# Hybrid attention and expert layer on one core: weights split earlier, squares moved a stage ahead, expert rows loaded ahead, h turned first

## The chip, the cores and the metric

The kernel runs on one core of one Trainium2 chip. The time is the device time of one execution in microseconds; the figure quoted is the median of the runs. One further execution was recorded by the hardware profiler, and every row below is from it.

## What is computed

One layer over 512 tokens of width 1024, in float32: a token mixer with two head groups and one output projection, then a retrieval of single-neuron experts. Cut to what matters here:

```python
h = rms(x) * (1 + scale1) + shift1
proj = h @ w_in
sb_out  = head_rms(stick_breaking_attention(...), 8 heads) * g_sb
gla_out = head_rms(gla_chunked(...), 4 heads) * g_gla * silu(g_r)     # gated linear attention
mixed = concatenate([sb_out, gla_out]) @ w_out
x = x + gate1 * mixed
h2 = rms(x) * (1 + scale2) + shift2
q = h2 @ w_peer_q                        # 8 heads x (128 + 128)
s1, s2 = q1 . keys_a, q2 . keys_b        # 128 keys each; top 16 of each, then top 16 of the pairs
act = gelu(h2 . expert_u[idx]);  y = sum(gates * act * expert_v[idx])
x = x + gate2 * y;  out = rms(x) * g_final
```

128 tokens get their experts by gathered rows; for the other 384 all 16384 expert rows are multiplied (128 blocks of 128 rows), and the picked ones are weighted.

## The kernel before

All data lie transposed in SBUF: 128 partitions of channels by 512 tokens, eight channel blocks (KD = 8, TB = 4 of them from each head group). Matrix products are made in three passes on a split of each float32 operand: hi is the value rounded to the matmul type fp32r, lo the remainder, and the passes are hi*hi, hi*lo, lo*hi. Every split costs a copy on ScalarE (hi) and a subtraction on VectorE or GpSimd (lo).

Every engine has its own queue, written out by hand in program order; engines meet by semaphores. The front of the kernel is a chain of blocks (`nc.Block()`), and all engines meet at the end of each. Around the change they are:

- stick-breaking attention (to 273 us), whose SyncE queue loads all of w_out (L623).
- `gated_linear` (273.7 to 295): TensorE sums squares of the attention output (`head_sums`, L817) for its norm, makes chunk scores (L827), state updates (L847) and outputs (L858, L864). ScalarE makes four squares, four logarithms (L774) and four exponentials (L777) for the norm; a third head sum has to wait for the first logarithm, as there are two banks. VectorE masks scores (L789), keeps the state, and at the end copies the four gated outputs from PSUM to catT (L809). GpSimd makes the mask.
- `mixer_back` (295 to 373): norm of the gated outputs (ScalarE squares L920, TensorE sums L975, ScalarE Ln and Exp L926, L928, VectorE L1020 and the gate L1022), then hi and lo of the concatenation (L923, L930, L934; `cat_low`, L1012), then the output projection: eight tiles n of eight blocks k of three matmuls (L986 to L988), tiles 0 and 1 interleaved by halves (`spans`). Its weights are split tile by tile into a ring of three buffers, hi by ScalarE (`w_high`, L917), lo by GpSimd (L966). VectorE adds each tile to x (L1029), ScalarE squares it (L943), VectorE adds the squares up (L1035, L1038). At the end the sum over channels (L994, L996), Ln and Exp (L948, L950), then for each k: VectorE scales (L1044), ScalarE makes h_hi (L955) and a full copy (L958), VectorE h_lo (L1048). TensorE then makes the first head's two query halves (L1002 to L1004), for which GpSimd splits the weights (L969) behind ScalarE's hi (L946, L951). These weights are loaded into the spent front of catT when cat_lo is done (L907).
- `retrieval` (373 on), within one block with everything that follows: SyncE loads keys, the first two expert blocks, the next query weights, more expert blocks (a ring of four, `UpProducts.load`, L1078). TensorE makes the key scores (L1297), turns the first 128 tokens of h (L1305, L1306), and then walks through 128 expert blocks (`product`, 24 matmuls each, L1103 to L1105), with the next head's query product (`query_of`, L1285) and scores between them. An expert block's hi is ScalarE's (L1086), its lo VectorE's (L1093, before VectorE's top-16 turn for blocks 0 and 1, within the turns for the others). GpSimd splits the next query weights (L1271) when the scores of the head before are copied (L1339), and then gathers expert rows for the indices that the turn has found (L1162).

The projections' buffer t16 has 16 slots of 512 columns. Slots 0 to 11 (queries and keys of both head groups) are spent when the gated stage's operands are made; slots 12 to 15 hold the gate, read at L1022.

## Time and profile before

| | us |
|---|---|
| median of three runs | 1639.35 |
| range of the runs | 1638.86 to 1641.07 |
| the profiled execution | 1643.19 |
| its span in the trace | 1641.5 |

| engine | busy us | share of the span |
|---|---|---|
| TensorE matmul (PE) | 1563.1 | 95% |
| TensorE weight load (PEld) | 1376.5 | 84% |
| VectorE (DVE) | 1290.5 | 79% |
| ScalarE (ACT) | 713.9 | 43% |
| GpSimd (POOL) | 392.6 | 24% |

How to read it: rows of a timeline give the start, the duration, the engine, the line of the kernel, the operation with out<-in, shape and count, and in brackets how long the engine had been idle and who ended that.
### The profile page before, as it was taken

How to read it: one execution, taken by the hardware profiler on the slowest of the kernel's cores; microseconds unless marked ns; L12 is line 12 of the kernel's file. 1: busy time of each engine (PE TensorE's matmuls, PEld its weight loads, DVE VectorE, ACT ScalarE, POOL GpSimd, SP SyncE). 2: the span in 40 equal slices, each digit the busy share in tenths (PEclk: the TensorE clock that was granted, in tenths of full speed). 3: DMA queues.
4: the chain of work that ended last, by engine and by line, in shares of the span. 5: the costliest groups of instructions: out<-in, count | busy, mean ns of one | idle time of the engine just before them, and what ended most of it. 6: DMA issues, size and time to landing. Idle time of an engine off the chain costs nothing.

```text
span 1641.5 us, 23626 instructions
## 1 busy us (share of the span) xinstructions
PE 1563.1 (95%) x8161; PEld 1376.5 (84%) x8161; DVE 1290.5 (79%) x2612; ACT 713.9 (43%) x1124; POOL 392.6 (24%) x328
## 2 busy tenths in 40 slices
PE   5899988889999999999999999999999999999996
PEld 3687656668899999999999999998888888888885
DVE  6665375546598999999999999747888888888888
ACT  4222384443343434334477677634333333333333
POOL 0000000321432333233222222102333333333330
PEclk8899988999999999999999999999999999999998
DMA  8573300005768887888889899879999999999992
GB/s 318 210 276 146 116 14 0 27 0 198 273 206 270 284 278 241 286 256 279 288 268 319 317 325 318 320 254 335 343 350 358 352 356 356 354 351 356 350 358 94
DMA packets 176963, 426.83 MB, mean 260 GB/s; under 512 B 15168, under 2 KB 99280, under 8 KB 172112
## 3 DMA queue, kind: packets, MB, share of 16 engines
q1 hardware_dynamic: 139984, 291.14, 50.7%
q0 software_dynamic: 36864, 134.23, 23.7%
q8 instruction: 63, 1.03, 0.2%
q14 instruction: 52, 0.43, 0.1%
HBM read 372.88 MB, written 52.43 MB: 259 GB/s over the span
## 4 chain that ended last, share of the span: by engine, by line
PE 72%; DVE 1%; issue 0%; ACT 0%; DVEq 0%; ACTq 0%
PE ps_y L1886 10%; PE ps_y L1888 10%; PE ps_y L1890 10%; PE ps_u L1103 10%; PE ps_u L1105 10%; PE ps_u L1104 10%; PE ps_g L1598 5%; PE ps_q L1285 1%; PE ps_q L1287 1%; PE ps_q L1286 1%; PE ps_s L1297 1%; DVE y_scaled L1861 0%; DVE row L1868 0%; PE ps_u L1910 0%; DVE y_row L1182 0%
## 5 line engine op out<-in xcount | busy, mean ns | idle before, releaser
L1103 PE MATMUL ps_u<-h_hi,u_hi 128*128 128x384 f32 x1024 | 348.8, 341 | 1.7 <-DVE u_lo L1093 1.7
L1105 PE MATMUL ps_u<-h_hi,u_lo 128*128 128x384 f32 x1024 | 345.0, 337 | 0.0
L1104 PE MATMUL ps_u<-h_lo,u_hi 128*128 128x384 f32 x1024 | 344.8, 337 | 0.0
L1765 ACT CAST v_hi<-v_raw 128x1024 fp32r<-128x1024 f32 x128 | 134.7, 1052 | 327.4 <-issue 327.4
L1162 POOL DMA_INDIRECT row<-in_v,row_index x128 | 176.8, 1381 | 401.5 <-DVE y_row L1182 308.0
L1162 POOL DMA_INDIRECT row<-in_u_rows,row_index x128 | 151.0, 1180 | 448.3 <-DVE row_dots L1169 377.6
L1822 DVE TENSOR_TENSOR v_lo<-v_raw,v_hi 128x1024 fp32r<-128x1024 f32 x128 | 160.6, 1255 | 103.2 <-ACT v_hi L1765 103.2
L1886 PE MATMUL ps_y<-v_hi,w_hi 128*128 128x512 f32 x768 | 237.3, 390 | 0.0
L1888 PE MATMUL ps_y<-v_lo,w_hi 128*128 128x512 f32 x768 | 236.6, 389 | 0.0
L1890 PE MATMUL ps_y<-v_hi,w_lo 128*128 128x512 f32 x768 | 236.5, 389 | 0.0
L1093 DVE TENSOR_TENSOR u_lo<-u_raw,u_hi 128x1024 fp32r<-128x1024 f32 x128 | 167.0, 1311 | 78.1 <-ACT u_hi L1086 78.0
L1103 PEld LDWEIGHTS ps_u<-h_hi,u_hi 128*128 128x128 f32 x1024 | 193.3, 189 | 2.4 <-DVE u_lo L1093 1.8
L1104 PEld LDWEIGHTS ps_u<-h_lo,u_hi 128*128 128x128 f32 x1024 | 193.1, 189 | 0.6
L1105 PEld LDWEIGHTS ps_u<-h_hi,u_lo 128*128 128x128 f32 x1024 | 193.0, 188 | 0.0
L1890 PEld LDWEIGHTS ps_y<-v_hi,w_lo 128*128 128x128 f32 x768 | 144.1, 188 | 30.1
L1888 PEld LDWEIGHTS ps_y<-v_lo,w_hi 128*128 128x128 f32 x768 | 144.1, 188 | 30.1
L1886 PEld LDWEIGHTS ps_y<-v_hi,w_hi 128*128 128x128 f32 x768 | 143.4, 188 | 29.2
L1113 ACT ACTIVATE u_act<-ps_u 128x384 f32<-128x384 f32 x128 | 62.8, 490 | 232.4 <-PE ps_u L1105 221.9
L1182 DVE SCALAR_TENSOR_TENSOR y_row<-row,row_weights,y_row 128x1024 f32<-128x1024 f32 x126 | 160.6, 1276 | 0.0
L1169 DVE CUSTOM_DVE_ANT_0 row<-row,h_row 128x1024 f32<-128x1024 f32 x128 | 155.3, 1217 | 1.8 <-DMA row<-in_u_rows,row_index 1.8
L1086 ACT CAST u_hi<-u_raw 128x1024 fp32r<-128x1024 f32 x128 | 134.1, 1048 | 3.2 <-DMA u_raw<-in_u 3.2
L1598 PE MATMUL ps_g<-hot_i,hot_j 128*128 128x128 f32 x768 | 91.9, 275 | 0.0
(284 smaller groups left out, 2325.9 us busy)
## 6 DMA issues: line engine op xcount, KB each, us to landing
u_raw<-in_u SPq DMA_DIRECT2D x128, 512.0 KB
v_raw<-in_v SPq DMA_DIRECT2D x128, 512.0 KB
w_ada<-in_w_ada SPq DMA_DIRECT2D x24, 1024.0 KB, 6.4
activations<-u_act SPq DMA_DIRECT2D x128, 192.0 KB
gate_tiles<-g_tile SPq DMA_DIRECT2D x12, 2048.0 KB
gates<-gate_tiles SPq DMA_DIRECT2D x32, 768.0 KB
act<-activations SPq DMA_DIRECT2D x128, 192.0 KB
w_proj<-in_w_proj SPq DMA_DIRECT2D x16, 512.0 KB, 3.9
```

Of the source, the lines that this page charges most:

```text
L1093: dve.tensor_tensor(self.lo[n][:], self.raw[n][:], self.hi[n][:].bitcast(F32), ALU.subtract).then_inc(self.lo_done, 1)
L1103: pe.matmul(out, self.hi[n][:, k], hi, start=(k == 0), stop=False)
L1104: pe.matmul(out, self.hi[n][:, k], lo, start=False, stop=False)
L1105: last = pe.matmul(out, self.lo[n][:, k], hi, start=False, stop=(k == KD - 1))
L1162: pool.indirect_dma_start(out=self.row[n][:], out_offset=None, in_=self.table[q // PICKS], in_offset=bass.IndirectOffsetOnAxis(ap=self.ind ...
L1169: dve.tensor_tensor_reduce(self.row[n][:], self.row[n][:], h_row[:], 1.0, 0.0, ALU.mult, ALU.add, self.dots[:, q:q + 1])\
L1182: dve.scalar_tensor_tensor(y, self.row[n][:], col, y, ALU.mult, ALU.add).then_inc(self.row_used, 1)
L1598: last = pe.matmul(ps_g[m][:, o], hot_j[x % HB][:, slot], hot_i[x % HB][:, slot], start=True, stop=True)
L1822: dve.tensor_tensor(v_lo[i % VS][:], v_raw[i % VS][:], v_hi[i % VS][:].bitcast(F32), ALU.subtract).then_inc(vlo, 1)
L1886: pe.matmul(out, hi, v_hi[i % VS][:, c], start=first, stop=False)
L1888: pe.matmul(out, hi, v_lo[i % VS][:, c], start=False, stop=False)
L1890: last = pe.matmul(out, lo, v_hi[i % VS][:, c], start=False, stop=end)
```

## The change

- **Two weight tiles split ahead.** Eight buffers of one weight tile each (`keep["split"]`) are laid over t16. In `gated_linear`, ScalarE copies the hi of out-projection tiles 0 and 1 between its squares and its logarithms, GpSimd subtracts their lo. `mixer_back` uses these four buffers as its ring, which has two places now instead of three; tile n's hi waits for product n - 2.
- **Squares a stage earlier.** ScalarE squares the gated outputs from PSUM at the end of `gated_linear`, two before and two after VectorE's copies of the same banks, and VectorE copies heads 2 and 3 first.
- **First query weights.** Their hi and lo go into buffers 4 to 7. ScalarE's copies stand in tiles 2 and 3 of the projection, and the lo is VectorE's now, not GpSimd's.
- **Order of the query product.** Per k the two hi*hi and lo*hi pairs wait for h_hi alone; the pair with h_lo follows.
- **cat_low(2, 4)** comes behind the first gated channel on VectorE.
- **Expert blocks 0 to 3** are loaded in `mixer_back`, behind the query weights in SyncE's queue; in `retrieval` the next query weights directly follow the keys.
- **h turned first**, before the first scores; ScalarE makes the hi of expert blocks 0 and 1 before it copies the scores.

```diff
         ps_o = [pb(f"ps_gla_o{h}", [P, T]) for h in range(GLA_HEADS)]
-        zeros = sem("gla_block_zeros")
+        w_hi, w_lo = keep["split"][0:2], keep["split"][2:4]
+        zeros, whi, squared, o_kept = sem("gla_block_zeros"), sem("w_out_first_hi"), sem("gla_o_squared"), sem("gla_o_kept")
...
             pool.memset(causal[0:C, C:P], 0.0).then_inc(zeros, 1)
+            for n in range(2):
+                pool.wait_ge(whi, n + 1)
+                pool.tensor_tensor(w_lo[n][:], keep["w_out"][:, n], w_hi[n][:].bitcast(F32), ALU.subtract)
...
                 act.activation(sq[:, c], catT[:, c], ACT.Square).then_inc(sq_done, 1)
+            act.wait_ge(keep["w_out_in"], 16)
+            for n in range(2):
+                act.copy(w_hi[n][:], keep["w_out"][:, n]).then_inc(whi, 1)
...
                 act.activation(rstd[:, c], rstd[:, c], ACT.Exp, scale=-0.5).then_inc(rstd_done, 1)
+            for p in range(GLA_PAIRS):
+                if p == 0:
+                    act.wait_ge(o_done, 2)
+                else:
+                    act.wait_ge(o_kept, 2)
+                for h in (2 * p, 2 * p + 1):
+                    act.activation(v8[:, 0, h], ps_o[h][:], ACT.Square).then_inc(squared, 1)
...
                     dve.scalar_tensor_tensor(catT[:, n], catT[:, n], keep["gains"][:, n:n + 1], rstd[:, n], ALU.mult, ALU.mult)
-            for h in range(GLA_HEADS):
-                dve.wait_ge(o_done, h // 2 * 2 + 2)
-                dve.tensor_copy(catT[:, TB + h], ps_o[h][:])
+            for p in reversed(range(GLA_PAIRS)):
+                if p == 0:
+                    dve.wait_ge(squared, 2)
+                else:
+                    dve.wait_ge(o_done, GLA_HEADS)
+                for h in (2 * p, 2 * p + 1):
+                    dve.tensor_copy(catT[:, TB + h], ps_o[h][:]).then_inc(o_kept, 1)
...
-def mixer_back(nc, io, keep, t16, v8, gx, catT, query):
+def mixer_back(nc, io, keep, t16, v8, gx, catT, query, up):
...
         h_hi, h_lo = keep["h_hi"], keep["h_lo"]
-        WS = 3
+        WS = 2
...
         cat_hi, cat_lo = sb("cat_hi", [P, KD, T], F32R), sb("cat_lo", [P, KD, T], F32R)
-        w_hi = [sb(f"w_out_hi{n}", [P, KD, P], F32R) for n in range(WS)]
-        w_lo = [sb(f"w_out_lo{n}", [P, KD, P], F32R) for n in range(WS)]
+        w_hi, w_lo = keep["split"][0:2], keep["split"][2:4]
...
         halves = lambda tile: [tile[:, 2 * s:2 * s + 2].rearrange("p a (b c) -> p (a b) c", c=P) for s in range(2)]
-        wq, wq_hi, wq_lo = halves(catT), halves(cat_hi), halves(cat_lo)
+        wq = halves(catT)
+        wq_hi, wq_lo = [keep["split"][n] for n in (4, 6)], [keep["split"][n] for n in (5, 7)]
...
         ps_x = pb("ps_sum_2", [P, T])
-        sq_done, sum_done, ln_done, rstd_done = sem("hsq"), sem("hsum"), sem("hln"), sem("hrstd")
+        sum_done, ln_done, rstd_done = sem("hsum"), sem("hln"), sem("hrstd")
...
                 sp.dma_start(wq[s], io["w_q"][s]).then_inc(wq_in, 16)
+            for b in range(up.RING):
+                up.load(sp, b)
...
             def w_high(n):
-                if n == 0:
-                    act.wait_ge(keep["w_out_in"], 16)
-                if n >= WS:
-                    act.wait_ge(mix_done, n - WS + 1)
-                    act.wait_ge(wlo, n - WS + 1)
+                act.wait_ge(mix_done, n - WS + 1)
...
-            for c in range(NG):
-                act.activation(sq[:, c], catT[:, TB + c], ACT.Square).then_inc(sq_done, 1)
-                if c == 1:
-                    w_high(0)
-                    act.copy(cat_hi[:, 0:2], catT[:, 0:2]).then_inc(chi, 2)
+            act.copy(cat_hi[:, 0:2], catT[:, 0:2]).then_inc(chi, 2)
...
                     act.copy(cat_hi[:, 2:4], catT[:, 2:4]).then_inc(chi, 2)
-                    w_high(1)
...
             for n in range(KD):
-                if n + 2 < KD:
-                    w_high(n + 2)
+                if n + WS < KD:
+                    w_high(n + WS)
...
                 act.activation(sq[:, n % 2], xT[:, n], ACT.Square).then_inc(sq2_done, 1)
-            act.wait_ge(wq_in, 32)
-            act.wait_ge(mix_done, KD)
-            act.copy(wq_hi[0], wq[0]).then_inc(query["hi"], 1)
+                if 2 <= n < 4:
+                    act.wait_ge(wq_in, 32)
+                    act.copy(wq_hi[n - 2][:], wq[n - 2]).then_inc(query["hi"], 1)
...
             act.activation(rstd[:, 0], rstd[:, 0], ACT.Exp, scale=-0.5).then_inc(rstd2_done, 1)
-            act.copy(wq_hi[1], wq[1]).then_inc(query["hi"], 1)
...
         def _(pool):
-            for n in range(KD):
-                pool.wait_ge(whi, n + 1)
-                if n >= WS:
-                    pool.wait_ge(mix_done, n - WS + 1)
+            for n in range(WS, KD):
+                pool.wait_ge(whi, n - WS + 1)
+                pool.wait_ge(mix_done, n - WS + 1)
                 pool.tensor_tensor(w_lo[n % WS][:], keep["w_out"][:, n], w_hi[n % WS][:].bitcast(F32), ALU.subtract).then_inc(wlo, 1)
-            for s in range(2):
-                pool.wait_ge(query["hi"], s + 1)
-                pool.tensor_tensor(wq_lo[s], wq[s], wq_hi[s].bitcast(F32), ALU.subtract).then_inc(query["lo"], 1)
...
             for c in range(NG):
-                pe.wait_ge(sq_done, c + 1)
...
             for n, k0, k1 in spans:
-                pe.wait_ge(wlo, n + 1)
+                if n >= WS:
+                    pe.wait_ge(wlo, n - WS + 1)
...
             for k in range(KD):
-                pe.wait_ge(lo_done, k + 1)
+                pe.wait_ge(hi_done, k + 1)
...
                     pe.matmul(bank[:], wq_hi[s][:, k], h_hi[:, k], start=(k == 0), stop=False)
-                    pe.matmul(bank[:], wq_hi[s][:, k], h_lo[:, k], start=False, stop=False)
-                    last = pe.matmul(bank[:], wq_lo[s][:, k], h_hi[:, k], start=False, stop=(k == KD - 1))
+                    pe.matmul(bank[:], wq_lo[s][:, k], h_hi[:, k], start=False, stop=False)
+                pe.wait_ge(lo_done, k + 1)
+                for s in range(2):
+                    last = pe.matmul(query["ps"][s][:], wq_hi[s][:, k], h_lo[:, k], start=False, stop=(k == KD - 1))
...
             cat_low(0, 2)
-            cat_low(2, 4)
...
                 dve.tensor_tensor(catT[:, at], catT[:, at], t16[:, GLR + c], ALU.mult).then_inc(cat_done, 1)
-                if c >= 1:
+                if c == 0:
+                    cat_low(2, 4)
+                else:
...
                     dve.tensor_tensor(total, total, sq[:, n % 2], ALU.add).then_inc(added, 1)
+                if 2 <= n < 4:
+                    dve.wait_ge(query["hi"], n - 1)
+                    dve.tensor_tensor(wq_lo[n - 2][:], wq[n - 2], wq_hi[n - 2][:].bitcast(F32), ALU.subtract).then_inc(query["lo"], 1)
...
         self.raw = [sb(f"u_raw{n}", [P, KD, P]) for n in span]
+        self.act = [sb(f"u_act{n}", [P, DENSE]) for n in span]
+        self.u_in, self.stored = [sem(f"u_in{n}") for n in span], [sem(f"act_stored{n}") for n in span]
+        self.hi_done, self.lo_done, self.mul, self.act_done = sem("u_hi_done"), sem("u_lo_done"), sem("u_mul"), sem("u_act_done")
+
+    def open(self, nc, ctx):
+
+        span = range(self.RING)
...
         self.hi, self.lo = [split(f"u_hi{n}") for n in span], [split(f"u_lo{n}") for n in span]
-        self.act = [sb(f"u_act{n}", [P, DENSE]) for n in span]
         self.ps = [ctx.enter_context(nc.psum_tensor(f"ps_u{n}", [P, T], F32)) for n in range(2)]
-        self.u_in, self.stored = [sem(f"u_in{n}") for n in span], [sem(f"act_stored{n}") for n in span]
-        self.hi_done, self.lo_done, self.mul, self.act_done = sem("u_hi_done"), sem("u_lo_done"), sem("u_mul"), sem("u_act_done")
...
             load_keys(0)
-            for b in range(2):
-                up.load(sp, b)
             load_query(1)
-            for b in range(2, up.DEEP):
+            for b in range(up.RING, up.DEEP):
...
-            scores_of(0)
...
                 last.then_inc(h_turned, 1)
+            scores_of(0)
...
                 keep_query(0, s)
+            for b in range(up.AHEAD - 1):
+                up.high(act, b)
             keep_scores(0)
-            for b in range(up.AHEAD):
-                up.high(act, b)
+            up.high(act, up.AHEAD - 1)
...
                 keep[n] = msb(n, [P, P], d)
-            t16, v8, gx = msb("t16", [P, N_PROJ, T]), msb("v8", [P, 2, TB, T]), msb("gate_x", [P, GLA_PAIRS, T])
+            t16 = msb("t16", [P, N_PROJ, T])
+            t16_at = nc.sbuf_top
+            v8, gx = msb("v8", [P, 2, TB, T]), msb("gate_x", [P, GLA_PAIRS, T])
+            keep["split"] = [nc.alloc_sbuf_tensor_at(f"w_split{n}", [P, KD, P], F32R, offset=t16_at + n * 4 * KD * P) for n in range(8)]
...
             }
-            mixer_back(nc, io, keep, t16, v8, gx, catT, query)
-        acts = nc.dram_tensor("activations", [N_KEYS, P, DENSE], F32, kind="Internal").ap()
+            acts = nc.dram_tensor("activations", [N_KEYS, P, DENSE], F32, kind="Internal").ap()
+            up = UpProducts(nc, top, io, keep, acts)
+            mixer_back(nc, io, keep, t16, v8, gx, catT, query, up)
         g_stored = [top.enter_context(nc.semaphore(f"g_stored{n}")) for n in range(2)]
-        up = UpProducts(nc, top, io, keep, acts)
+        up.open(nc, top)
```

## Rows read from the trace of the kernel before

**Rows 1.** the page, part 4: the chain that ended last, share of the span by engine

```profile
PE 72%; DVE 1%; issue 0%; ACT 0%; DVEq 0%; ACTq 0%
```

**Rows 2.** TensorE's waits from 381 us on: engine, line, waited for: us, times, longest

```profile
PE ps_q L1285 <- POOL w_query_lo L1271: 3.8, 1, 3.8
PE ps_g L1582 <- DVE g_tile L1553: 2.0, 1, 2.0
```

**Rows 3.** timeline of TensorE, gated stage to first expert product

```profile
277.56 1.98 PE L817 MATMUL ps_upd<-sq_sb,pair_ones 128*128 128x512 f32 x4
...
296.02 3.52 PE L975 MATMUL ps_hs<-v,ones 128*128 128x512 f32 x4 [3.30 <-ACT v L920]
...
312.48 0.52 PE L986 MATMUL ps_mix<-cat_hi,w_out_hi 128*128 128x512 f32 x1 [1.03 <-DVE cat_lo L1012]
...
350.94 1.02 PE L994 MATMUL ps_sum<-gate_x,ones 128*128 128x512 f32 x2
...
359.95 0.77 PE L1002 MATMUL ps_q<-h_hi,cat_hi 128*128 128x512 f32 x1 [6.23 <-DVE h_lo L1048]
...
375.28 2.02 PE L1297 MATMUL ps_s<-keys,query 128*128 128x128 f32 x16 [2.28 <-DMA keys<-in_keys_a]
...
380.74 0.44 PE L1103 MATMUL ps_u<-h_hi,u_hi 128*128 128x384 f32 x1 [1.70 <-DVE u_lo L1093]
```

**Rows 4.** timeline of ScalarE

```profile
275.83 1.44 ACT L774 ACTIVATE rstd_sb<-ps_upd,eps 128x512 f32<-128x512 f32 x2
...
296.39 1.03 ACT L917 CAST w_out_hi<-w_out_raw 128x1024 fp32r<-128x1024 f32 x1
...
356.49 0.72 ACT L955 ACTIVATE h_hi<-v,mod 128x512 fp32r<-128x512 f32 x1 [0.44 <-DVE v L1044]
...
373.30 1.07 ACT L1332 COPY query<-ps_q 128x512 f32<-128x512 f32 x2 [4.44 <-PEq L876]
```

**Rows 5.** timeline of VectorE

```profile
298.47 2.47 DVE L1012 TENSOR_TENSOR cat_lo<-catT,cat_hi 128x1024 fp32r<-128x1024 f32 x1 [3.41 <-ACT cat_hi L923]
...
310.35 0.74 DVE L1020 SCALAR_TENSOR_TENSOR catT<-catT,gains,v 128x512 f32<-128x512 f32 x1
...
318.49 0.75 DVE L1029 SCALAR_TENSOR_TENSOR xT<-ps_mix,mod,xT 128x512 f32<-128x512 f32 x1 [1.45 <-PE ps_mix L988]
...
355.15 4.06 DVE L1044 SCALAR_TENSOR_TENSOR v<-xT,mod,v 128x512 f32<-128x512 f32 x2 [3.26 <-ACT v L950]
...
407.72 1.23 DVE L1093 TENSOR_TENSOR u_lo<-u_raw,u_hi 128x1024 fp32r<-128x1024 f32 x1 [2.42 <-ACT u_hi L1086]
```

**Rows 6.** timeline of GpSimd

```profile
297.51 2.36 POOL L966 TENSOR_TENSOR w_out_lo<-w_out_raw,w_out_hi 128x1024 fp32r<-128x1024 f32 x1 [23.02 <-ACT w_out_hi L917]
...
317.60 2.40 POOL L966 TENSOR_TENSOR w_out_lo<-w_out_raw,w_out_hi 128x1024 fp32r<-128x1024 f32 x1 [1.72 <-ACT w_out_hi L917]
...
356.13 2.53 POOL L969 TENSOR_TENSOR cat_lo<-catT,cat_hi 128x1024 fp32r<-128x1024 f32 x1 [0.22 <-ACT cat_hi L951]
...
385.75 5.64 POOL L1271 TENSOR_TENSOR w_query_lo<-w_query,w_query_hi 128x1024 fp32r<-128x1024 f32 x2 [10.36 <-issue]
...
430.11 4.68 POOL L1271 TENSOR_TENSOR w_query_lo<-w_query,w_query_hi 128x1024 fp32r<-128x1024 f32 x2
```

**Rows 7.** stretches: from:to length, busy us (instructions) per engine, granted clock, DMA, GB/s

```profile
312.40:351.00 38.60, 38.52 (x163) 31.70 (x164) 10.55 (x16) 10.14 (x14) 14.36 (x6) 0.96 0.08 28
360.00:373.00 13.00, 13.00 (x48) 10.28 (x48) 8.37 (x13) 8.38 (x13) 0.00 (x0) 0.85 0.00 1
373.00:381.00 8.00, 4.02 (x33) 3.91 (x34) 1.77 (x3) 4.14 (x6) 2.10 (x24) 1.00 0.77 272
381.00:385.00 4.00, 4.00 (x15) 4.00 (x15) 3.97 (x22) 1.38 (x2) 0.00 (x0) 0.57 1.02 411
```

**Rows 8.** DMA issues: the first query weights, size, median us to landing

```profile
catT<-in_w_q SPq DMA_DIRECT2D x2, 512.0 KB, 3.7
```

**Rows 9.** VectorE's waits from 500 to 600 us

```profile
DVE u_lo L1093 <- ACT u_hi L1086: 8.2, 4, 2.6
```

## The prediction, made before the changed kernel was run

> **What bounds the kernel now.** I read the page's chain of waits first: TensorE holds 72% of it and the other engines 1% or less [rows 1]. Next TensorE's waits from 381 us to the end: in 1260 us it stands still for another engine only three times, for 3.8 us, 2.0 us [rows 2] and, at 380.7 us, 1.7 us [rows 3]. So behind the first expert product a microsecond saved earlier is a microsecond saved at the end, unless one of those waits grows. The change works in front of that point, and there the timeline of TensorE shows the holes: 3.30 us before the head sums at 296.02, 1.03 us before 312.48, 6.23 us before 359.95, 2.28 us before 375.28 and 1.70 us before 380.74 [rows 3]. The third view is the granted clock by stretch: 0.96 of 38.6 us, 0.85 of 13 us, 0.57 of 4 us [rows 7]. The clock has two levels, 1.2 and 2.4 GHz; the share missing times the length is what the lower one costs: 1.5, 1.95 and 1.7 us. Each of these slow stretches begins just behind or inside such holes.
>
> All steps below are on the clock of the profiled execution.
>
> **Gated stage: ScalarE gets two weight copies ahead of its logarithms.** A copy of 128x1024 takes 1.03 us (L917 [rows 4]). The four squares end at 275.83, where the first logarithm starts now [rows 4]; with two copies ahead it starts at 277.85 and ends 0.7 us later, at 278.55. TensorE's third head sum waits for it and ran at 277.56 [rows 3], so it is 1.0 us late, and the rest of the stage follows in one chain (sum, logarithm, second scores, masks, state updates). **+1.0 us**, from both sides: 0 if TensorE had slack there (the row shows none), 2.0 if the whole ScalarE delay came through. The weights themselves are loaded a stage earlier (line 623). The four squares of the gated outputs go into ScalarE's empty tail: before, four DVE copies ended the stage; now two copies, two more copies beside two squares, with ScalarE starting two squares ahead. Two 128x512 reads of PSUM take 1.07 us (L1332 [rows 4]), so four in two rounds end within 0.1 us of the old end. Cost 0; with the swap of banks serial it would be 0.5 us.
>
> GpSimd splits two weights (2.36 us each [rows 6]) from 276.9 to 281.7, beside VectorE's masks. Does that hold VectorE up? With two SBUF operands, yes: cat_lo at 298.47 took 2.47 us beside GpSimd's 2.36 us from 297.51, and the same form takes 1.23 us alone (407.72) [rows 5, 6]. With one operand in PSUM, no: L1029 at 318.49 took 0.75 us, no longer than the all-SBUF form of the same size alone (310.35, 0.74 us), though GpSimd was splitting a weight beside it [rows 5]. The masks read PSUM, the catT gains (SBUF alone) come after 283. Cost 0, or up to 2.4 us as a rival.
> The Trainium skill (SBUF — State Buffer, section "SBUF: two separate sides") says the same of the shared port pair: an exclusive lock, held for the whole instruction, which a VectorE instruction needs against GpSimd if it has two SBUF inputs or runs in a two-port mode. By that rule too the masks are free, while the 4.06 us below are such a lock, so the sum is the same with and without it.
>
> **Normalising and the first half of the product.** The stage starts 1.0 us later, near 296.35. The head sums need no squares of their own stage now and start with it, but still at the low clock: 3.52 us for the first two [rows 3], then half of that for the other two; they end at 301.7. ScalarE's queue has lost four squares and two weight copies (4 x 0.6 + 2 x 1.03): its last exponential, paced by the sums now, ends at 304.2. VectorE does cat_low(0,2) unblocked in 1.23 us. A gated channel costs it three instructions of 512 columns, 0.74 us the first (310.35 [rows 5]) and some 0.65 us each of the others (half of 1.23 us): 2.0 us. In the new queue the first gated channel is done at 300.95, cat_low(2,4) at 302.15, the second at 303.55, the first gated cat_low at 305.45 (behind ScalarE's copy at 304.15), and two channels later, 309.45, TensorE can start its block k=6 of tile 0. Before this is the row at 312.48. **-3.0 us**, the +1.0 above already in it.
>
> From there 162 matmuls (6 + 12 + 6 x 24) lie before 350.94 [rows 3]: 38.46 us, less 1.5 us for the clock, is 0.228 us each, 36.9 us. TensorE's holes shrink from 2.3 us in the last four before 312.5 to about 1, so I take the slow stretch as gone: **-1.5 us**. New is the ring of two: tile 2 needs slot 0, so its copy starts when tile 0 ends (311.0), ScalarE 1.04 us, GpSimd 2.4 us: 314.5. TensorE would be ready at 313.7. **+0.85 us**. Later tiles take 24 x 0.228 = 5.45 us each and the rebuild 3.5 us, so 1.9 us are spare; the cover is tile n+1's own product. VectorE's adds of squares, behind GpSimd until +4 us, and the query-weight remainder (1.23 us) behind them end at about +5.3 us of 5.45 in tiles 2 and 3. If that slipped, three product banks hide it. ScalarE's wait for the query weights stands in its queue before the copies for tile 5 and on: they are issued at 310.2 and took 3.7 us before [rows 8]; needed at 320.4, so 6 us are spare even with the four expert loads behind them (2 MB more). Those loads wait for nothing and nobody waits for them here. Product end: 347.2 instead of 350.94, **-3.7 us in all** (-3.0 -1.5 +0.85).
>
> **From the product to the query product.** Sums, logarithm and exponential keep their length. Then VectorE's first two scalings took 4.06 us (L1044 [rows 5]): the GpSimd split of query weights (356.13, 2.53 us [rows 6]) held them; unheld they take 0.75 us each, so h_hi(0) starts at 355.9 instead of 356.49 [rows 4]. And TensorE no longer waits for h_lo(0) but for h_hi(0): it starts at 356.7 instead of 359.95 [rows 3]. **-3.25 us.** Does the feed keep up? ScalarE gives a channel each 1.42 us (two instructions of 0.7 us like 356.49 [rows 4]), TensorE takes 6 x 0.228 = 1.37 us at full clock, but loses 1.95 us at the low clock first [rows 7], so it stays behind the feed and its end moves with its start. If the clock stayed high across the shorter hole (3 us instead of 6.2), the feed would bind and 1.6 us more would be won.
>
> **From the query product to the experts.** The stage starts at t = 373.3 before. Turning h first: VectorE's cast ends at +0.3, 16 matmuls of the kind that took 2.02 us (L1297 [rows 3]) end at +2.2; the keys land at +2.0 as before; scores end at +4.0. Expert rows 0 and 1 lie there already: ScalarE does the query copies (1.07 us), u_hi(0), u_hi(1) (to +3.1); VectorE takes u_hi(0) at +2.1, GpSimd's small index patterns being done by then, and ends u_lo(0) at +3.35 (1.23 us [rows 5]). So the first product starts at +4.0, not at +7.44 (380.74): **-3.45 us**. u_lo(1) at +4.6 is needed at +8.3. And with no hole from +0.3 on the slow stretch of 381 to 385 should go: **-1.7 us**. ScalarE behind it: scores copied at +5.1, u_hi(2), then query weights, loaded 1 MB earlier in SP's queue; GpSimd's halves (5.64 us for two [rows 6]) are done by +12.6, the first needed at +12.5 is done at +9.8.
>
> **What is late next.** The wait of 3.8 us at 432 is for GpSimd's third pair of halves (430.11 [rows 6]), which stand behind eight row gathers, which wait for VectorE's first top-16 turn. TensorE comes there 12.1 us earlier; does VectorE? It starts the turn when the scores are copied, 3.4 us earlier within the stage, not 5.15 us as TensorE. But inside the turn it stood 2.42 us for u_hi (407.72 [rows 5]), which TensorE's second query product releases. It has to make up 1.7 us and has 2.4 us for it; then turn, gathers and wait move with TensorE, and the wait stays 3.8 us. GpSimd's halves may hold one u_lo meanwhile, by 0 to 1.2 us (the lock above, half a split).
>
> **Sum:** -3.7 -3.25 -3.45 -1.7 = **-12.1 us**; I take 12.0. The profiled execution took 1643.19 us (span 1641.5, 1.7 around it), 3.8 us above the median 1639.35; its own forecast is 1631.2, the median's 1627.3.
>
> **Rivals.**
> (a) The clock doesn't follow: one or both slow stretches (312 and 381) stay, as the new holes at 309 and 314 lie as close together. Speaks for it: each hole of 3 us and more in the rows is followed by one. Against: the stretch 373 to 381, with 2.28 us and 1.70 us of holes in it, ran at the high clock itself [rows 3, 7], and 381 to 385 paid for both together. Gain 8.8 to 10.5: **1628.9 to 1630.6**.
> (b) VectorE's first turn or GpSimd in front of it binds (held u_lo, masks held in the gated stage): the wait at 432 grows by 1 to 2.4 us: **1628.3 to 1629.7**.
> (c) Gain swallowed: VectorE, which makes the top-16 turns, a remainder per expert block and the row products, turns out to pace the kernel from its first turn by itself, and what TensorE gains it waits again at L1582, where it already waits 2.0 us [rows 2]: about **1638**. Against: VectorE stands idle for ScalarE's u_hi again and again, 8.2 us between 500 and 600 us [rows 9], and ScalarE waits for TensorE there, so VectorE is fed by TensorE's pace.
> (d) Slower: the ring of two. If GpSimd's split grew, because VectorE's two-operand instructions now fall beside every split, from 2.4 to over 4.3 us, each of the tiles 3 to 7 would wait; to eat 12 us the rebuild must exceed a tile by 2.5 us, that is a split of 6.8 us; with the low clock that such holes bring, 5.8 us. At 7.5 us: about **1643**. Against: the longest split beside a busy VectorE took 2.8 us on average (385.75 [rows 6]).
> (e) Parts not doing what they say: the loads ahead are plain queue order and the waits removed are gone in the diff; what remains is that the keys land later behind 2 MB of loads. Those end near 320, so no.
>
> **How the numbers follow.** Forecast 0.64; (a) 0.19; (b) 0.10; (c) 0.04; (d) 0.02; 0.01 for a clock that stays high. A measurement of this kernel can tell about 0.2%, 3.3 us. Faster 0.94, same 0.04, slower 0.02. The low end is the sum with the low clock of the query product gone as well (-1.6) and 1 us of scatter: 1624.7; the high end is (a) with both stretches plus the +1 of (b): 1631.6, and 0.9 us for holes of the +1.0 kind that the rows don't show: 1632.5.
>
> **What would show it.** Third head sum about 1 us later; L1012 at 1.23 us; block k=6 near 309.5 and tile 2 behind a wait of under 1 us for GpSimd, none for tiles 3 to 7; product end near 347.2; the two L1044 at 0.75 us; query product 3 us behind the sums; first expert product 4 us behind the stage's start at clock 1.0; the wait at L1285 still near 3.8 us, at about 420. I am wrong if a wait for w_out_lo repeats per tile, if the clock row 0.57 only moves, or if L1285's wait grows past 5 us.

## The result, and the profile after

| | before | after |
|---|---|---|
| median, us | 1639.35 | 1631.96 |
| range of the runs | 1637.39 to 1642.65 (11) | 1626.81 to 1636.67 (10) |
| the profiled execution | 1643.19 | 1631.97 |
| its span | 1641.5 | 1630.2 |

The ratio is 0.9949, with a 95% interval of 0.9936 to 0.9962 (6.2 to 10.5 us). By the medians the change takes off 7.4 us where 12.0 were forecast. The time lies in the range (1624.7 to 1632.5), near its upper end. After scatters over 10 us, and with it the clock: the run of 1626.81 us had a mean granted clock of 0.983, that of 1636.67 us 0.974. An eleventh run of after took 1973.81 us at a mean granted clock of 0.745; it is counted in the median alone, neither in the range nor in the ratio.

First, what is not the change's. The kernel up to `gated_linear` is the same in both, but TensorE's first matmul of that stage starts at 273.76 us before and at 268.71 after. Over the profiles of all kernels here this start lies anywhere between 268.7 and 274.8. So I measure from it (**t0**). Span minus t0 is 1367.7 before and 1361.5 after: 6.2 us are won behind t0, and 5.05 of the 11.2 us between the two spans are scatter of the front.

TensorE's timeline of after, for the places of [rows 3] (start, duration, then idle before and who ended it):

```profile
291.50 3.50 PE L980 MATMUL ps_hs<-v,ones 128*128 128x512 f32 x4 [2.88 <-PEq L736]
...
304.87 0.50 PE L992 MATMUL ps_mix<-cat_hi,w_split 128*128 128x512 f32 x1 [1.02 <-DVE cat_lo L1020]
...
310.23 0.50 PE L992 MATMUL ps_mix<-cat_hi,w_split 128*128 128x512 f32 x1 [0.81 <-POOL w_split L975]
...
344.05 1.02 PE L1000 MATMUL ps_sum<-gate_x,ones 128*128 128x512 f32 x2
...
349.92 0.76 PE L1008 MATMUL ps_q<-h_hi,w_split 128*128 128x512 f32 x1 [3.07 <-ACT h_hi L965]
...
364.77 0.33 PE L1318 MATMUL ps_h<-ident_r,h_hi 128*128 128x128 f32 x1 [0.60 <-DVE ident_r L1380]
...
366.61 2.00 PE L1311 MATMUL ps_s<-keys,query 128*128 128x128 f32 x16
368.37 0.42 PE L1119 MATMUL ps_u<-h_hi,u_hi 128*128 128x384 f32 x1
...
418.21 0.80 PE L1299 MATMUL ps_q<-h_hi,w_query_hi 128*128 128x512 f32 x1 [3.40 <-POOL w_query_lo L1285]
```

The holes went as meant: 1.02 us for a cat_lo, one wait of 0.81 us for the ring, 3.07 us before the query product where there were 6.23, and none before the first expert product. Put side by side from t0, each column being the step's own length:

| step, us | before | after | moved by | forecast |
|---|---|---|---|---|
| t0 to the end of the projection | 77.18 | 75.34 | -1.84 | -3.7 |
| from there to the query product | 9.01 | 5.87 | -3.14 | -3.25 |
| query product | 13.35 | 14.54 | +1.19 | 0 |
| its end to the first expert product | 7.44 | 3.91 | -3.53 | -3.45 |
| slow stretch behind it | | | -1.62 | -1.7 |

Here 8.9 us are won. 6.2 arrive at the end, so some 2.7 are given back later. The stretches show where. After (from:to, length, busy us and instructions of PE, PEld, DVE, ACT, POOL, then the granted clock, DMA share, GB/s):

```profile
304.80:344.00 39.20, 38.32 (x162) 30.44 (x163) 22.61 (x18) 12.17 (x16) 14.42 (x6) 1.00 0.22 81
350.00:364.00 14.00, 14.00 (x48) 10.91 (x48) 9.25 (x14) 9.43 (x15) 0.00 (x0) 0.78 0.01 1
368.00:372.00 4.00, 4.00 (x27) 4.00 (x26) 3.11 (x14) 3.35 (x5) 0.24 (x1) 1.00 0.94 317
411.00:426.00 15.00, 11.60 (x44) 9.69 (x44) 7.72 (x33) 4.43 (x6) 11.06 (x6) 0.77 0.91 321
795.00:825.00 30.00, 28.04 (x176) 27.72 (x175) 25.91 (x55) 18.80 (x38) 3.14 (x4) 0.94 0.58 178
```

The last two of them in the kernel before:

```profile
425.00:440.00 15.00, 11.20 (x49) 9.49 (x48) 8.02 (x35) 4.54 (x7) 11.36 (x6) 0.89 0.86 312
805.00:835.00 30.00, 28.04 (x183) 27.72 (x182) 27.57 (x57) 19.98 (x39) 3.31 (x3) 1.00 0.69 214
```

The slow stretches of [rows 7] at 312 and at 381 are gone (1.00 and 1.00). The one behind the wait for GpSimd is twice as long (6.8 us instead of 3.4; +1.0 us by the marks around it), and at 800 us, where both kernels wait 2.0 us for VectorE's g_tile, after has a slow stretch (0.06 of 30 us is 1.8) and before has none. From the gated stage on, both profiles spend 20.5 us at the lower clock, their last 12 us left aside.

The slow stretch at the query product costs more than before (0.78 of 14 us is 3.1 us lost; 0.85 of 13 us was 1.95), but it isn't longer. It lasts 6.8 us in both; before:

```profile
357.20:364.00 6.80, 4.04 (x10) 3.24 (x11) 6.53 (x9) 5.22 (x10) 1.46 (x1) 0.50 0.01 2
```

and after:

```profile
349.25:356.05 6.80, 6.13 (x15) 4.81 (x16) 5.79 (x10) 6.45 (x11) 0.00 (x0) 0.50 0.01 2
```

Before, TensorE stood still in 2.8 us of it, waiting for h_lo; now it starts early enough to run 6.1 us of the product at half the clock.

### The profile page after: what moved, and what is told of

It is laid out like the page before. It is cut to its first block, busy times and chain, and to the rows that moved or that the text cites. A ratio compares the mean times of both kernels' runs of the same rounds, so it can differ in the third digit from the quotient of the medians.

```text
span 1630.2 us, 23619 instructions
## 1 busy us (share of the span) xinstructions
PE 1556.7 (95%) x8161; PEld 1372.2 (84%) x8161; DVE 1296.5 (80%) x2614; ACT 713.4 (44%) x1124; POOL 385.5 (24%) x326
## 4 chain that ended last, share of the span: by engine, by line
PE 72%; DVE 1%; issue 0%; ACT 0%; DVEq 0%; ACTq 0%
PE ps_y L1901 10%; PE ps_y L1903 10%; PE ps_y L1905 10%; PE ps_u L1119 10%; PE ps_u L1121 10%; PE ps_u L1120 10%; PE ps_g L1613 5%; PE ps_q L1299 1%; PE ps_q L1300 1%; PE ps_q L1301 1%; PE ps_s L1311 1%; DVE y_scaled L1876 0%; DVE row L1883 0%; PE ps_u L1925 0%; DVE y_row L1198 0%
```

## The experiments

Two questions came from the table. Why does the projection take longer per matmul? And is the clock's share given back for good? The letters A and B in a quoted expectation are the two rival explanations of that run alone.

### The place of the weight tiles

Between 304.87 and 344.05 TensorE hardly waits, and its clock is 1.00, yet the 162 matmuls take longer. The timelines of TensorE in the middle of a tile, before:

```profile
328.49 0.39 PE L986 MATMUL ps_mix<-cat_hi,w_out_hi 128*128 128x512 f32 x1
...
330.76 0.39 PE L987 MATMUL ps_mix<-cat_lo,w_out_hi 128*128 128x512 f32 x1
```

and after:

```profile
316.65 0.40 PE L992 MATMUL ps_mix<-cat_hi,w_split 128*128 128x512 f32 x1
...
318.99 0.39 PE L993 MATMUL ps_mix<-cat_lo,w_split 128*128 128x512 f32 x1
```

The two rows of each pair lie ten matmuls apart: 0.227 us from start to start before, 0.234 after. Over a whole tile it is 0.2272 and 0.2342, and 162 x 0.0070 is 1.1 us. The split tiles lie in t16 now, at other addresses than the old ring. My first theory was that their start modulo 64 bytes decides; the rival, that something else at the new place or beside it does.

**a1_align_mix** puts 32 bytes before t16:

```diff
+            msb("t16_pad", [P, 8], F32)
             t16 = msb("t16", [P, N_PROJ, T])
```

> The changed kernel with 32 bytes of padding in front of the projections' buffer t16, so that the eight split tiles laid over it (and what lies below it on that side: v8, w_out, catT) start at a multiple of 64 bytes instead of 32 past one. In the changed kernel the matmuls of the output projection and the first query product follow each other every 0.2345 us, before the change every 0.2275 us. Theory A (the start address of the weight tiles modulo 64 costs it): spacing back to 0.2275 us in both, about 1.3 us less in the projection and 0.3 us in the query product, the median some 1.6 us below the changed kernel's 1632. Theory B (the place at that end of SBUF, or the writes of the ring beside it, cost it, not the alignment): spacing stays 0.2345 us and the median stays within scatter. Expert products stay at 0.1775 us by both.

Measured: 1633.55 us, 0.9954 [0.9938, 0.9971], spacing 0.2333. The address moves the spacing, but only from 0.2342 to 0.2333: modulo 64 is not the rule. The median, forecast 1.6 us below after's, is 1.6 us above it, inside the scatter.

**a2_align_u** puts the same 32 bytes before the expert splits instead; **a3_align_both** has both.

```diff
+        self.splits.enter_context(nc.sbuf_tensor("u_pad", [P, 8], F32, side="right"))
         self.hi, self.lo = [split(f"u_hi{n}") for n in span], [split(f"u_lo{n}") for n in span]
```

> The changed kernel with the 32 bytes of padding in front of the expert blocks' split tiles (u_hi, u_lo) alone: they too start 32 bytes past a multiple of 64. Their matmuls have 384 columns and follow each other every 0.1775 us. Theory A, if the 0.007 us hold for this shape too: spacing 0.1705 us over 3072 matmuls, about 21 us less; if less of it shows at 384 columns, in proportion. Theory B: 0.1775 us, no change of the time. The projection stays at 0.2345 us by both.

> Both paddings. Theory A: both spacings fall and the gains add, the median about 1.6 us below that of the run with the expert tiles alone. Theory B: nothing changes.

Measured: a2 1640.18 us, 0.9996 [0.9980, 1.0013]; a3 1639.32 us, 0.9992 [0.9974, 1.0010]. **Thirty-two bytes cost 8.2 us**, all that the whole change had won. The groups by line from 600 to 800 us (count, busy us, mean ns), after:

```profile
L1119 PE MATMUL ps_u<-h_hi,u_hi 128*128 128x384 f32 x327 | 110.1, 337 | 0.0
```

and a2_align_u:

```profile
L1120 PE MATMUL ps_u<-h_hi,u_hi 128*128 128x384 f32 x319 | 108.0, 339 | 0.0
```

The same 200 us hold 8 fewer of them, and from start to start it is 0.1761 us instead of 0.1734. Over 128 blocks of 24 matmuls: 3072 x 0.0027 = 8.3 us. The sign was the opposite of my expectation (which also gave the spacing as 0.1775 where it is 0.1734); the effect of the place is plain. In a3 both spacings are those of the single runs, 0.2333 and 0.1761.

**c2_ring_place** is the kernel before with nothing changed but the place: its ring of three lies over t16. (The lines that define `keep["split"]`, as in the change, are left out here.)

```diff
-        w_hi = [sb(f"w_out_hi{n}", [P, KD, P], F32R) for n in range(WS)]
-        w_lo = [sb(f"w_out_lo{n}", [P, KD, P], F32R) for n in range(WS)]
+        w_hi, w_lo = keep["split"][0:3], keep["split"][3:6]
```

> The kernel before with one edit: its ring of three split weight tiles lies over t16 (the same addresses as in the changed kernel), nothing else. If the place or start address of the weight tiles alone costs the spacing (theories A and B), the projection's matmuls follow each other every 0.2342 us instead of 0.2272, about 1.1 us more in the projection, while the first query product, whose tiles lie in cat_hi and cat_lo here, stays at 0.2275. If the place of cat_hi and cat_lo (moved up by 22 KB in the change) or the loads and the order of the change cost it, the spacing stays 0.2272.

Measured (a single run): 1640.99 us; spacing 0.2342, the projection ends 78.39 us behind t0 instead of 77.18. Ten matmuls of it:

```profile
328.66 0.39 PE L986 MATMUL ps_mix<-cat_lo,w_split 128*128 128x512 f32 x1
...
331.00 0.39 PE L987 MATMUL ps_mix<-cat_hi,w_split 128*128 128x512 f32 x1
```

So the place alone costs the 1.2 us: the spacing is after's to the last digit, without after's order or work beside it. The query product of c2, whose weights have kept their place, keeps its spacing too (0.2273).

**c1_pad96** has 96 bytes at both places, **d4_pad224** 224 bytes before t16 alone:

```diff
+            msb("t16_pad", [P, 24], F32)     # d4: [P, 56]
```

> The changed kernel with 96 bytes of padding in front of both t16 and the expert blocks' split tiles, so that weight tiles and the data they are multiplied with start at the same place modulo 512 (384), as the projection's did before the change. Theory A, mended after the last runs (not the start modulo 64, where 32 bytes made the expert matmuls slower, 0.1761 against 0.1734 us, but the start modulo 128 or the distance to the moving data costs it): projection spacing back to 0.2272 us (now 0.2342), expert spacing at 0.1704 us (0.2272/512 per column) or at least not above 0.1734; if 0.1704, 3072 x 0.003 = 9 us less. Theory B (the place at that end of SBUF): projection stays at 0.2342 us, expert spacing anywhere.

> The changed kernel with 224 bytes of padding in front of t16: the split tiles start at 256 modulo 512, so at a multiple of 128, but 128 bytes off the moving data's place (384). If the start modulo 128 is what counts: projection spacing 0.2272 us. If weights and moving data have to start alike modulo 256 or 512: 0.233 us or more.

Measured: c1 1629.85 us, 0.9931 [0.9907, 0.9955]; spacing 0.2274, the projection ends 74.28 us behind t0 (-1.06 against after); the experts at 0.1735, no better than after's 0.1734, so the gain hoped for there didn't come. Ten matmuls of c1's projection:

```profile
328.65 0.39 PE L992 MATMUL ps_mix<-cat_hi,w_split 128*128 128x512 f32 x1
...
330.92 0.39 PE L993 MATMUL ps_mix<-cat_lo,w_split 128*128 128x512 f32 x1
```

d4 (a single run): 1637.06 us, spacing 0.2324. c1 also rules out explanation B, that this end of SBUF as such is slow: 96 bytes further down it is fast. With the start addresses modulo 512 of the weight tiles (by the kernels' own allocation; the data that move through them start at 384 in all cases):

| 512 columns | weights start at | spacing, us |
|---|---|---|
| before's ring; c1 | 384 | 0.2272; 0.2274 |
| the projections of the front | 128 | 0.2278 |
| d4 | 256 | 0.2324 |
| a1 | 448 | 0.2333 |
| after, c2 | 480 | 0.2342 |

Fast are the cases in which weights and data start alike modulo 256. That is a description of six cases and no more: for the experts' 384 columns, starts of 480 and 384 give 0.1734 and 0.1735 and 448 gives 0.1761, which it doesn't explain. The pads before t16 also shift what lies below it (v8, w_out, catT); only c2 moves the ring alone. The rule stays open.

### The wait for GpSimd and the clock behind it

**r1_halves_first** lets GpSimd split the third pair of query weights after four of the eight row gathers, instead of after all.

```diff
-                if h < LAST:
+                if h < LAST and h != 1:
...
+                if h == 0:
+                    for r in range(4):
+                        rows.gather(pool, r)
+                    pool.wait_ge(s_copied, 4)
+                    query_low(2)
+                    for r in range(4, gathered(1)):
+                        rows.gather(pool, r)
+                    continue
```

> The changed kernel with GpSimd's halves of the third head's query weights put behind the fourth of its eight first row gathers instead of behind the eighth. In the changed kernel TensorE waits 3.4 us for them at 418 us and then runs 6.8 us at the low clock, which costs another 3.4 us. If that wait is only the order on GpSimd (theory A): the wait and the low stretch behind it vanish, 5 to 6.8 us less. If VectorE's first top-16 turn is what paces this place (theory B), its row dots wait for the later four gathers and the wait only moves: within 1.5 us of the changed kernel.

Measured: 1626.12 us, 0.9919 [0.9903, 0.9934], 5.8 us faster than after for a wait of 3.4. GpSimd's split, after first, then r1:

```profile
411.83 3.95 POOL L1178 DMA_INDIRECT row<-in_u_rows,row_index  x1 [0.30 <-issue]
415.80 4.69 POOL L1285 TENSOR_TENSOR w_query_lo<-w_query,w_query_hi 128x1024 fp32r<-128x1024 f32 x2
```

```profile
406.22 4.78 POOL L1285 TENSOR_TENSOR w_query_lo<-w_query,w_query_hi 128x1024 fp32r<-128x1024 f32 x2
```

It is done nearly ten microseconds earlier. In r1 TensorE's only wait left between 370 and 1620 us is the one for g_tile, and the clock stays up in both places:

```profile
410.00:425.00 15.00, 15.00 (x78) 13.64 (x77) 14.52 (x58) 6.05 (x8) 11.03 (x8) 1.00 0.96 358
785.00:815.00 30.00, 28.03 (x185) 27.71 (x184) 27.57 (x58) 20.22 (x40) 3.31 (x3) 1.00 0.66 206
```

The medians fall by 2.4 us more than the wait (5.8 - 3.4). The lower clock is the candidate: in after 6.1 us of the product behind the wait ran at it (418.2 to 424.3, clock 0.50), which is 3.1 us lost, and in r1 none. The stretch at 800 is gone too, though r1 holds the whole change and the same 2.0 us wait: so the change doesn't bring that stretch about by its own work.

a3's profile shows the same without a new order on GpSimd. There the last gather before the split took 1.57 us, where it took 3.95 to 3.97 in all ten others with the old order, and TensorE's wait shrank to 0.78 us:

```profile
416.42 1.57 POOL L1179 DMA_INDIRECT row<-in_u_rows,row_index  x1 [0.30 <-issue]
```

```profile
420.67 0.50 PE L1300 MATMUL ps_q<-h_hi,w_query_hi 128*128 128x512 f32 x1 [0.78 <-POOL w_query_lo L1286]
```

No slow stretch follows there (clock 1.00 from 415 to 425). So 2.4 of the 3.4 us are the length of one gather, and VectorE's timeline shows what it waits for. In after:

```profile
411.49 2.35 DVE L1109 TENSOR_TENSOR u_lo<-u_raw,u_hi 128x1024 fp32r<-128x1024 f32 x2
413.75 1.22 DVE L1185 CUSTOM_DVE_ANT_0 row<-row,h_row 128x1024 f32<-128x1024 f32 x1
```

The gather begins 0.3 us behind the first of these three instructions, each with two operands in SBUF, and ends 0.8 us behind the last one, at 415.78. All 13 gathers of 3.9 us and more here, one for each profile but a3, have the same three beside them and end the same 0.8 us behind them. In a3 the gather ends 0.8 us behind the first of them (417.18), and GpSimd's split starts before the third. r1 too has the long gather (414.48, 3.93 us), but behind the split. That the gather is held by them is read from the times and not tested by an edit.

### The parts of the change undone

**d2_front_undone** takes back the early weight splits and the squares: ScalarE and GpSimd make them in `mixer_back` again (the ring of two and its place stay).

```diff
-            act.wait_ge(keep["w_out_in"], 16)
-            for n in range(2):
-                act.copy(w_hi[n][:], keep["w_out"][:, n]).then_inc(whi, 1)
...
+            for c in range(NG):
+                act.activation(sq[:, c], catT[:, TB + c], ACT.Square).then_inc(sq_done, 1)
+                if c == 1:
+                    w_high(0)
```

> The changed kernel with the part in the gated stage undone: squares and the first two weight splits back in the stage of the projection (the ring stays at two places in t16). By my sum the part costs 1.0 us in the gated stage and 0.85 us at tile 2, and gains 4.0 us before block k=6 and a slow stretch. Measured from the gated stage's first matmul, the projection ends at 75.3 us in the changed kernel: by the sum it ends at about 77.5 here if the clock stays high, 79 with a stretch at the low clock around 312, as before. Rival: the feed by VectorE's norm steps, not the splits, sets the pace of that stretch, and undoing the part costs under 1 us.

Measured: 1633.52 us, 0.9959 [0.9943, 0.9975], 1.6 us above after. The 1.6 us alone lie inside the intervals; the places in the profile carry the reading. The projection ends 77.29 us behind t0 (after 75.34), and TensorE waits twice for GpSimd's split there, one of the two in the first half:

```profile
302.80 0.50 PE L984 MATMUL ps_mix<-cat_hi,w_split 128*128 128x512 f32 x1 [0.58 <-POOL w_split L967]
...
314.02 0.50 PE L984 MATMUL ps_mix<-cat_hi,w_split 128*128 128x512 f32 x1 [0.80 <-POOL w_split L967]
```

The early splits and squares are worth 1.95 us at that point, though the smaller ring and the bad place are kept. At the first expert product 0.9 us of it is left, as the slow stretch at the query product lasted only 3.4 us in this profile. And the slow stretch at 312 doesn't come back (clock 1.00 from 300 to 340): all twelve profiles with the change or most of it lack it, before and c2 have it, so its going isn't shown to be the work of the early splits and squares.

**c3_query_undone** gives the first query weights' copies and subtractions back to their old places and engines, and TensorE waits for h_lo again.

```diff
-                if 2 <= n < 4:
-                    act.wait_ge(wq_in, 32)
-                    act.copy(wq_hi[n - 2][:], wq[n - 2]).then_inc(query["hi"], 1)
+            act.wait_ge(wq_in, 32)
+            act.copy(wq_hi[0][:], wq[0]).then_inc(query["hi"], 1)
...
-                pe.wait_ge(hi_done, k + 1)
+                pe.wait_ge(lo_done, k + 1)
```

> The changed kernel with the query weights' part undone: their hi copies behind the product again, their lo on GpSimd, TensorE waiting for h_lo before all three matmuls. By my sum this part is worth 3.25 us between product end and query product, by the lock between GpSimd and VectorE (the two first scalings take 4.06 us again, not 1.42) and by the earlier wait: the query product starts about 9.0 us behind the product's end, not 5.9, and the median is 3 us above the changed kernel's. Rival: the query product is fed by ScalarE's pace anyway, and the part is worth under 1 us.

Measured: 1633.53 us, 0.9963 [0.9945, 0.9981], 1.6 us above after, again inside the intervals. The timelines of VectorE, GpSimd and TensorE show the mechanism whole:

```profile
351.07 4.07 DVE L1054 SCALAR_TENSOR_TENSOR v<-xT,mod,v 128x512 f32<-128x512 f32 x2 [3.26 <-ACT v L960]
...
352.05 2.54 POOL L978 TENSOR_TENSOR w_split<-catT,w_split 128x1024 fp32r<-128x1024 f32 x1 [0.21 <-ACT w_split L961]
...
355.88 0.77 PE L1011 MATMUL ps_q<-h_hi,w_split 128*128 128x512 f32 x1 [6.24 <-DVE h_lo L1058]
```

The same two scalings in after:

```profile
348.26 1.42 DVE L1056 SCALAR_TENSOR_TENSOR v<-xT,mod,v 128x512 f32<-128x512 f32 x2 [3.26 <-ACT v L961]
```

The query product starts 9.02 us behind the projection instead of 5.87. But at the first expert product only 1.7 us of these 3.15 are left: from the product's start to the first turning of h it is 13.4 us, in after 14.9. The slow stretch says why. It lasts 6.8 us in both and starts 5.1 to 5.2 us behind the projection's end in both (351.9 here, 349.2 in after). With the longer hole 2.9 us of it fall on the product, in after 6.1; half of the difference is 1.6 us. So an earlier start inside a slow stretch won half of itself. My expectation of 3 us left that out.

**c4_experts_undone** loads the expert blocks in `retrieval` again, turns h behind the scores and copies the scores before u_hi.

```diff
-            for b in range(up.RING):
-                up.load(sp, b)
...
             load_keys(0)
+            for b in range(2):
+                up.load(sp, b)
             load_query(1)
...
+            scores_of(0)
             pe.wait_ge(ident_done, 1)
```

> The changed kernel with the expert part undone: blocks 0 and 1 loaded in the retrieval stage behind the keys, key scores before the turning of h, scores copied before the first expert hi. By my sum the first expert product starts 7.4 us behind the stage's start, not 4.0, and the clock row falls to its low level behind it: at the first GELU 5 us late. Theory A: those 5 us reach the end, the median is 4 to 5 us above the changed kernel's. Theory B: VectorE's first top-16 turn paces the wait at 418 us, so that part of it is taken back there: that wait shrinks below 3.4 us and the end moves by 3.4 us or less.

Measured: 1637.88 us, 0.9982 [0.9964, 1.0000]; 5.9 us above after, where 4 to 5 were expected, which the scatter allows. Both holes of [rows 3] and the slow stretch are back:

```profile
371.12 2.02 PE L1311 MATMUL ps_s<-keys,query 128*128 128x128 f32 x16 [2.21 <-DMA keys<-in_keys_a]
...
376.58 0.44 PE L1117 MATMUL ps_u<-h_hi,u_hi 128*128 128x384 f32 x1 [1.70 <-DVE u_lo L1107]
```

```profile
379.00:383.00 4.00, 4.00 (x20) 4.00 (x19) 3.97 (x26) 2.04 (x3) 0.00 (x0) 0.75 0.98 392
```

This is the largest part of the change: 5.9 us by the medians, where the other two make 1.6 each. TensorE's wait for the third query weights is 3.46 us with it undone, 3.40 with it: it moves with TensorE.

### A version that beats both

**d1_best** is r1_halves_first with the 96 bytes before t16. **d3_gaps** moves besides ScalarE's two w_out copies of the gated stage from before the logarithms to behind the second and the fourth one:

```diff
                 act.activation(rstd[:, c], ps_u[c % 2][:], ACT.Ln, bias=keep["eps"][:], scale=1.0 / SB_DH).then_inc(ln_done, 1)
+                if c == 1:
+                    act.wait_ge(keep["w_out_in"], 16)
+                if c % 2:
+                    act.copy(w_hi[c // 2][:], keep["w_out"][:, c // 2]).then_inc(whi, 1)
```

> The changed kernel with both edits that gained: 96 bytes of padding in front of t16 and the third head's weight halves behind the fourth row gather. If the two are independent, as I expect: projection spacing 0.2274 us, no wait at the third head's query product, median 1.1 to 1.6 us below the run with the gathers reordered (1626.1), about 1624.8. Rival: the later stages take part of it back, same as 1626.

> As the combined kernel, with the two weight copies of the gated stage moved into ScalarE's own gaps: the first behind the second logarithm, the second behind the fourth. The third head sum no longer waits for the copies. By my reading of the +1.0 us step the stage behind starts 22.3 us after the gated stage's first matmul instead of 22.8, as before the change; GpSimd's second split then ends near VectorE's first SBUF-only instruction and holds it up by 0.4 us at most. Median 0.3 to 0.6 us below the combined kernel's. Rival: GpSimd's later splits hold VectorE's gains and state steps, and it is 1 us or more slower.

Measured: d1 1624.89 us, 0.9905 [0.9886, 0.9924], as expected; d3 **1623.51 us** (1622.97 to 1624.98), 0.9900 [0.9884, 0.9916]. In d3 the head sums of `mixer_back` start 21.85 us behind t0 (d1 22.80, before 22.26), and the projection ends at 72.73 (d1 74.35); of that 1.6 us the start explains 0.95. The rest need not be a merit of the edit: the slow stretch at the head sums lasts 6.8 us in d1's profile (296.7 to 303.5) and 3.4 us in d3's (294.2 to 297.6). In its timelines the copy fills a hole, and the split of GpSimd that follows it now falls beside a gain of VectorE with SBUF operands alone, which takes 1.16 us instead of 0.75:

```profile
275.11 1.03 ACT L781 CAST w_split<-w_out_raw 128x1024 fp32r<-128x1024 f32 x1
...
279.23 2.37 POOL L769 TENSOR_TENSOR w_split<-w_out_raw,w_split 128x1024 fp32r<-128x1024 f32 x1 [0.63 <-ACT w_split L781]
...
280.98 1.16 DVE L820 SCALAR_TENSOR_TENSOR catT<-catT,gains,rstd_sb 128x512 f32<-128x512 f32 x1
```

That 0.4 us lies off the chain. By the medians d3 is 1.4 us faster than d1, inside their intervals, so neither the 0.3 to 0.6 us expected nor more is shown; they are 16 and 14 us below before's.

## Why the prediction was right or wrong

**Gated stage, +1.0.** Right: the third head sum starts 3.80 us behind t0 before and 4.78 after. ScalarE's timeline in after, with the two copies ahead of the first logarithms:

```profile
268.69 2.19 ACT L774 ACTIVATE sq_sb<-catT 128x512 f32<-128x512 f32 x4 [3.46 <-PEq L597]
270.78 1.98 ACT L777 CAST w_split<-w_out_raw 128x1024 fp32r<-128x1024 f32 x2
272.67 1.25 ACT L781 ACTIVATE rstd_sb<-ps_upd,eps 128x512 f32<-128x512 f32 x2
```

ScalarE starts its first work of the next stage 1.18 us later from t0; the head sums only 0.53 us, since they don't wait for squares there. The first logarithm stands 4.0 us behind the start of the squares, with the copies' 1.98 us in it; d3, with the copies in the holes behind, gets the stage's end back.

**Cost of 0 for the masks beside GpSimd's splits.** Right, and with it the rule of the shared ports as drawn from the Trainium skill (SBUF — State Buffer, section "SBUF: two separate sides"): the first two masks, with one operand in PSUM, took 1.29 us in the middle of GpSimd's splits, as before without them. GpSimd and VectorE in after:

```profile
271.90 4.67 POOL L769 TENSOR_TENSOR w_split<-w_out_raw,w_split 128x1024 fp32r<-128x1024 f32 x2 [2.45 <-ACT w_split L777]
...
272.73 1.29 DVE L803 TENSOR_TENSOR gla_scores<-ps_gla_o,gla_causal 128x512 f32<-128x512 f32 x2 [2.07 <-PE ps_gla_o L845]
```

**Block k=6, -3.0.** Measured -2.56. The cat_lo subtraction took 1.22 us as forecast, unheld.

**First half's clock, -1.5; ring of two, +0.85.** Both right: clock 1.00, one wait of 0.81 us for GpSimd, none for tiles 3 to 7. Rival (d) is out. What took the slow stretch at 312 away isn't isolated, as d2 lacks it too.

**Projection end, -3.7.** Wrong, -1.84. The step that failed is "0.228 us each": I carried the spacing over from a row in which the weights lay elsewhere, and the diff says in plain words that they move. That is +1.1 (shown by c2 and c1). 0.44 comes from block k=6. The other 0.3 is for the most part what I had left out of the price of a wait: the matmul behind the 0.81 us of idle time starts 1.20 us after the one before it (309.03, 310.23), 0.97 more than the usual spacing and not 0.85, and the one behind that 0.10 late as well.

**Query product starts, -3.25.** Right, -3.14, and c3 undoes it. **The product itself, 0.** Wrong, +1.19. I took its loss to the slow stretch as fixed at 1.95 us, though that stretch begins inside the hole that the change shortens (357.2, product from 359.95 on); the stretch kept its 6.8 us, 6.1 of them fell on the product, and 3.1 us were lost. The place of the weights adds 48 x 0.0070 = 0.3 us here as well. The stretch's length is itself a draw: r1, the same program up to this point, had 3.4 us of it. I had only given the loss a chance to vanish (0.01), none to grow.

**Retrieval, -3.45; slow stretch of 381, -1.7.** Right, -3.53 and -1.62, and c4 undoes both. **The wait stays at 3.8.** Right, 3.40 us at 418, with the row gathers before GpSimd's halves as the reason (r1); one gather of 3.95 us made most of it (a3). Rival (b) is out.

**The sum.** Its -3.2 us of clock were the weak term. In the profiles they came at both places, so rival (a) in its own wording is out too; but after's total at the lower clock is the same 20.5 us as before's. Its time, 1628.9 to 1630.6, would have been the nearer one nonetheless: what I lacked was the case in which the slow stretches go where they were forecast to go and others cost more (0.78, 0.77, 0.94 above). Step by step (place, block k=6, price of the wait, start and length of the query product, the wait shorter by 0.4, the slow stretches at 411 and 795):

-12.1 +1.1 +0.44 +0.3 +0.1 +1.19 -0.4 +1.0 +1.73 = -6.6 us, where 6.2 us were measured behind t0.

That the time lies in the range is partly luck: the range's upper end was made of rivals (a) and (b), and neither happened; the place of the weights and the slow stretches elsewhere filled it instead. The profiled execution's own forecast, 1631.2 us, was met (1631.97) by luck alone, with 5 us of scatter from ahead of the change in it.

How much of the clock part is the change's is open. It differs from run to run of the same code, and one profile of each kernel doesn't settle it. The runs say a little more: the share of the clock that was missing, times the span, is 35.9 us on average over 66 runs of before and 32.8 over ten of after, 3.1 us less, give or take 3. So an average gain of the size that I had forecast is possible, and so is almost none.

## What to carry to other kernels

When buffers move, the matmul spacing is no constant: measure it from start to start in a stretch without waits, at the new place, before the rest is judged, as 32 bytes here cost as much as all the reordering won. A microsecond of TensorE's idle time is worth itself, but only half if the earlier start falls into a slow stretch (c3). What the clock adds beyond that comes and goes with stretches elsewhere, so it belongs in the range and not in the sum. And after a reordering, look for the next wait on another engine's queue order: eight gathers ahead of two subtractions were worth 5.8 us.

## What the runs showed of the hardware

- **Place of the weights.** The same 512-column matmul takes 0.2272 or 0.2342 us from start to start, a 384-column one 0.1734 or 0.1761, by where the weight tile starts, at a granted clock of 1.00 in both.
- **Shared access of VectorE and GpSimd.** Two scalings with all operands in SBUF: 4.07 us beside a split, 1.42 alone. Masks with one operand in PSUM: 1.29 us for two, beside a split and without one. New to me was that a plain copy from SBUF to SBUF (L1044) is held too, 2.19 us beside the split of tile 2 where it takes 0.43 us alone. The sum behind it (L1047) I had foreseen held; TensorE waits for neither. VectorE in after:

```profile
308.27 2.19 DVE L1044 COPY gate_x<-v 128x512 f32<-128x512 f32 x1 [0.87 <-ACT v L954]
...
317.76 2.47 DVE L1047 TENSOR_TENSOR gate_x<-gate_x,v 128x512 f32<-128x512 f32 x1 [0.86 <-ACT v L954]
```

- **A gather beside VectorE.** A row gather of GpSimd's took 3.93 to 3.97 us in 13 profiles, where the shortest take 0.94. Each began beside three VectorE instructions with two SBUF operands that follow each other without a gap, and ended 0.8 us behind the last.
- **The lower clock.** TensorE's wait for GpSimd at 418 to 433 took 3.3 to 4.2 us in ten of the 14 profiles, and the lower clock came with its end in each, for 3.4 or 6.8 us: the ten microseconds around its end ran at a mean clock of 0.66 to 0.83. With a wait of 0.78 us (a3) and with none (r1, d1, d3) it stayed at 1.00. Near 800 all 14 have a wait of 1.9 to 2.0 us; the lower clock came there in four (after, a3, d3, d4), for 3.4 us, and not in the other ten.
- **Half of an earlier start.** Of 3.15 us by which the query product starts earlier in after than in c3, 1.7 were left behind it, as both profiles have a slow stretch of 6.8 us there and 6.1 instead of 2.9 us of it fall on matmuls.
